# First attention of a two-block model: two of the convolution's four channel tiles move from VectorE to TensorE

## The reference, cut to what matters

```python
def conv_group(a, b, conv_w, conv_b, g_ln, b_ln):
    h = a * jax.nn.sigmoid(b)
    h = lax.conv_general_dilated(h, conv_w[:, None, :].astype(h.dtype), window_strides=(1,),
                                 padding=[(CONV_K - 1, 0)],
                                 dimension_numbers=('NWC', 'WIO', 'NWC'),
                                 feature_group_count=CONV_CH) + conv_b
    h = layernorm(h, g_ln, b_ln)
    return jax.nn.silu(h)
```

## Time and profile before

| what | us |
|---|---|
| three runs | 3038.69, 3042.77, 3051.34 |
| their median | 3042.77 |
| the profiled execution | 3043.8 |
| its span, first to last instruction | 3042.0 |
| mean granted TensorE clock | 0.955 |
| PE, DVE, ACT, POOL busy | 2918.6, 1798.2, 996.2, 989.8 |

### The profile page before, as it was taken

One profiled execution on the slowest core, in us unless ns is written; L12 is line 12 of the kernel. 1 busy time (PEld: TensorE's weight loads), 2 busy tenths in 40 slices (PEclk: granted clock), 3 DMA queues, 4 the chain that ended last, 5 costly groups with the idle time before them and its releaser, 6 DMA issues. The chain is left out here.

```text
span 3042.0 us, 39382 instructions
## 1 busy us (share of the span) xinstructions
PE 2918.6 (96%) x15042; PEld 2590.3 (85%) x15042; DVE 1798.2 (59%) x3227; ACT 996.2 (33%) x1582; POOL 989.8 (33%) x611
## 2 busy tenths in 40 slices
PE   8787999999999999999999999999999899999998
PEld 7555799999998999999998787888788898778886
DVE  6785876989798587888885833331043455333311
ACT  4345233343433322222223223222223456332222
POOL 3201500111202232233343544444432344454442
PEclk9766999999999999999999999999999799999999
DMA  3101256696969988989984322333331000223332
GB/s 133 32 1 35 84 155 202 214 289 192 288 205 297 358 317 317 329 320 324 325 320 138 101 93 83 97 97 100 96 130 37 4 1 15 76 83 97 97 104 70
DMA packets 195744, 475.83 MB, mean 156 GB/s; under 512 B 17204, under 2 KB 104116, under 8 KB 193252
## 3 DMA queue, kind: packets, MB, share of 16 engines
q1 hardware_dynamic: 167764, 370.54, 37.0%
q0 software_dynamic: 27648, 100.68, 9.6%
q10 hardware_dynamic: 144, 2.10, 0.2%
HBM read 415.47 MB, written 56.62 MB: 155 GB/s over the span
## 5 line engine op out<-in xcount | busy, mean ns | idle before, releaser
L262 ACT ACTIVATE w_hi<-w 128x1024 fp32r<-128x1024 f32 (+2 forms) x485 | 506.6, 1046 | 1235.9 <-DVE ffn_gates L2127 326.0
L272 POOL TENSOR_TENSOR w_lo<-w,w_hi 128x1024 fp32r<-128x1024 f32 (+2 forms) x229 | 542.9, 2383 | 698.0 <-ACT w_hi L262 698.0
L272 DVE TENSOR_TENSOR w_lo<-w,w_hi 128x1024 fp32r<-128x1024 f32 x256 | 313.5, 1225 | 177.5 <-ACT w_hi L262 150.5
L307 PE MATMUL peer_psum<-xn_hi,w_hi 128*128 128x416 f32 x1024 | 366.3, 358 | 1.7 <-ACT peer_act_out L1629 1.7
L307 PE MATMUL peer_psum<-peer_w_hi,w_hi 128*128 128x416 f32 x1024 | 359.6, 351 | 1.8 <-DVE peer_w_lo L404 1.1
L308 PE MATMUL peer_psum<-xn_lo,w_hi 128*128 128x416 f32 x1024 | 360.9, 352 | 0.0
L309 PE MATMUL peer_psum<-xn_hi,w_lo 128*128 128x416 f32 x1024 | 360.7, 352 | 0.0
L308 PE MATMUL peer_psum<-peer_w_lo,w_hi 128*128 128x416 f32 x1024 | 358.6, 350 | 0.0
L309 PE MATMUL peer_psum<-peer_w_hi,w_lo 128*128 128x416 f32 x1024 | 358.6, 350 | 0.0
L1465 POOL DMA_INDIRECT peer_gathered<-in_peer_u,peer_chosen_here x96 | 140.9, 1468 | 644.5 <-DVEq L1712 515.3
L307 PE MATMUL ffn_psum<-ffn_hn_hi,w_hi 128*128 128x512 f32 x704 | 277.2, 394 | 10.7 <-DVE ffn_hn_lo L617 6.6
(11 more groups left out here) (417 smaller groups left out, 5727.9 us busy)
## 6 DMA issues: line engine op xcount, KB each, us to landing
w<-in_peer_uT SPq DMA_DIRECT2D x128, 512.0 KB, 4.1
w<-in_peer_v SPq DMA_DIRECT2D x128, 512.0 KB, 5.5
w<-in_f_w_gu SPq DMA_DIRECT2D x88, 512.0 KB, 3.5
peer_act<-peer_act_out SPq DMA_DIRECT2D x128, 208.0 KB, 5.2
peer_gate<-peer_gates_out SPq DMA_DIRECT2D x26, 1024.0 KB, 7.8
peer_gates<-peer_gate SPq DMA_DIRECT2D x16, 1664.0 KB, 9.5
peer_act_in<-peer_act SPq DMA_DIRECT2D x128, 208.0 KB, 4.5
w<-in_f_w_down SPq DMA_DIRECT2D x32, 512.0 KB, 3.5
```

The costliest lines, as they stand in the source:

```text
L262: act.activation(self.hi[:, x, 0:c], self.buf[:, x, 0:c], ACT.Copy).then_inc(self.rounded, 1)
L272: eng.tensor_tensor(self.lo[:, x, 0:c], self.buf[:, x, 0:c], self.hi[:, x, 0:c].bitcast(F32), ALU.subtract).then_inc(self.split, 1)
L307: pe.matmul(out, w[0], x[0], start=start, stop=False)
```

## The change

Channel tiles 3 and 2 are taken from DVE. For each tap k of each, POOL makes a 128x128 matrix with the tap's weights on the diagonal (identity times weight per partition) into one of 8 buffers `diag`; PE multiplies it with the shifted input and accumulates the 31 taps of a tile in PSUM bank 6, all in fp32. Tile 3 comes first, tile 2 after it in the same bank.

- On PE the taps stand between the scores and the transposes of a step (`ahead`): three a step up to step 10, where the 31st is one alone, none in step 11, four a step from step 12 to 18 and three in step 19. Each waits for its diagonal (`diag_made`); tap 31, the first of the second tile, also for the eviction of the first (`tile_taken`).
- On POOL the 62 diagonals stand ahead of its two additions; from the ninth on each waits until the matmul 8 before it has run (`diag_used`).
- On DVE `take` moves the sum from bank 6 to the accumulator and adds the bias, in step 11 and in step 20. `Conv.run` leaves tiles 2 and 3 alone, in both stages. The front still does 25 taps, on tiles 0 and 1; 37 are left for this stage, so `per_step` is 2.

```diff
--- before.py
+++ after.py
@@ -653,7 +653,7 @@
     def run(self, dve, own, m, there=CT):
 
         for _ in range(m):
-            left = [c for c in range(there) if self.taps[c] < CK]
+            left = [c for c in range(min(there, CT - 2)) if self.taps[c] < CK]
             if not left:
                 return
             c = left[sum(self.taps) % len(left)]
@@ -970,7 +970,7 @@
         for i, it in enumerate(items):
             self.last[it["bank"]] = i
 
-    def on_pe(self, pe, between=None):
+    def on_pe(self, pe, between=None, ahead=None):
         it, s, n_items = self.items, self.s, len(self.items)
         for n in range(n_items + self.lag + 1):
             if n < n_items:
@@ -981,6 +981,8 @@
                     mm = pe.matmul(self.S[n % len(self.S)][:, col:col + keys.shape[-1]], x["q"], keys,
                                    start=True, stop=True)
                 mm.then_inc(s["scored"], 1)
+            if ahead is not None:
+                ahead(n)
             if self.lag <= n < n_items + self.lag:
                 m = n - self.lag
                 x = it[m]
@@ -1117,8 +1119,13 @@
                   lambda j: kit.gain("g_out_conv", j), ps[:, 6:7, :], 1, need=(silu_done, lambda j: j + 1),
                   bufs=ln.bufs)
         own_sem, conv_sem = st.sem("vector_steps"), st.sem("conv_steps")
+        DIAGS, on_tensor = 8, [(c, k) for c in (CT - 1, CT - 2) for k in range(CK)]
+        diag = st.sb("tap_diagonals", [P, DIAGS, P])
+        diag_made, diag_used = st.sem("diagonals_made"), st.sem("diagonals_used")
+        tile_taken = st.sem("tile_taken")
         conv_steps = 20
-        per_step = -(-(CK * CT - sum(conv.taps)) // conv_steps)
+        per_step = -(-(CK * (CT - 2) - sum(conv.taps)) // conv_steps)
+        assert conv.taps[CT - 1] == conv.taps[CT - 2] == 0
         first = conv_steps + 1
         with nc.Block() as block:
 
@@ -1136,11 +1143,30 @@
                     pe.wait_ge(centred, 1)
                     ln.on_pe(pe)
 
+                def tap(n):
+                    c, k = on_tensor[n]
+                    pe.wait_ge(diag_made, n + 1)
+                    if n == CK:
+                        pe.wait_ge(tile_taken, 1)
+                    pe.matmul(ps[:, 6, :], diag[:, n % DIAGS, :], io["conv_in"][:, c, NMETA + k:NMETA + k + SEQ],
+                              start=(k == 0), stop=(k == CK - 1)).then_inc(diag_used, 1)
+
                 steps = {first: mean, first + 4: sum_ln, first + 10: sum_cn}
-                at.on_pe(pe, lambda n: steps[n]() if n in steps else None)
+
+                def some_taps(n):
+                    done = 3 * n if n < 12 else CK + 4 * (n - 12)
+                    for k in range(done, min(done + 3, CK) if n < 12 else min(done + 4, 2 * CK)):
+                        tap(k)
+
+                at.on_pe(pe, lambda n: steps[n]() if n in steps else None, some_taps)
 
             @block.gpsimd
             def _(pool):
+                for n, (c, k) in enumerate(on_tensor):
+                    if n >= DIAGS:
+                        pool.wait_ge(diag_used, n - DIAGS + 1)
+                    pool.tensor_scalar(diag[:, n % DIAGS, :], kit.ident[:, :], kit.gain("conv_w", k * CT + c), None,
+                                       ALU.mult).then_inc(diag_made, 1)
                 pool.wait_ge(rows_squared, 2)
                 pool.tensor_tensor(io["attn_sum"][:, :], squares[:, 0, :], squares[:, 1, :], ALU.add).then_inc(rows_added, 1)
                 pool.wait_ge(rows_squared, 3)
@@ -1188,11 +1214,20 @@
                          first + 11: lambda: cn.variance(dve), first + 13: factor,
                          first + 14: lambda: cn.scale(dve, own, cn.src, cn.gain, None, cn.out)}
 
+                def take(i):
+                    c = on_tensor[i * CK][0]
+                    dve.wait_ge(diag_used, CK * (i + 1))
+                    dve.tensor_scalar(acc[:, c, :], ps[:, 6, :], kit.gain("conv_b", c), None, ALU.add).then_inc(tile_taken, 1)
+
                 def between(n):
+                    if n == 11:
+                        take(0)
                     if n < conv_steps:
                         conv.run(dve, taps, per_step)
                     if n == conv_steps:
                         taps.wait()
+                        take(1)
+                        dve.wait_ge(tile_taken, 2)
                         for c in range(1, CT):
                             if c > 1:
                                 dve.wait_ge(conv_done, c - 1)
```

## The result

The kernel after took 3055.66 us (median of 19 runs, 3046.91 to 3063.88), the kernel before 3041.22 us (19 runs on the same chips, 3032.59 to 3051.34). The ratio is 1.0047, with a 95% interval from 1.0036 to 1.0057: 14.4 us slower. The forecast was 17 us slower; its time of 3061 is 5 us above the measured one. The outcome lies just inside the 0.5% that the prediction called no change, so its likeliest class, slower by more than that, was missed by a hair, and the interval reaches across that line. One slow execution each of two later kernels (3527.56 us of "eight diagonals", 3686.82 us of "half the columns") is left out of their medians and ratios.

The account below looks back on a forecast made before the run. DVE's taps were taken to bound the first attention, PE at full clock afterwards. Taps 55.8 + attention 46.4 + 3 - 4 put score matmul 20 22.9 us later; less 5.9 behind it, +17 us: 3061 us, range 3045 to 3095.

Parts of the forecast that it names:

- likeliest class: Whole program: slower by more than about 0.5% (15 us), chance 0.66; same 0.28, faster 0.06.
- The bound changes sides: First attention to score matmul 20: 42 us leave DVE, which stops being the bound, and PE becomes it.
- The tap: One 128x128 by 512 fp32 matmul on PE at full clock: 0.90 us, 62 of them 55.8 us, bounds 53.0 and 58.9.
- Attention beside the taps: PE's attention until score matmul 20: about 18.3 steps of 2.54 us at full clock, 46.4 us.
- The start at half clock: First steps of the attention: full clock only from the second or third step on, costing 3 us more.
- the weight load in front of a short group: PE in steps to 20: a long tap ahead can hide a load of about 0.19 us; 4 us off, 0 to 8.
- The clock: PE in the attention with taps: full clock from the second or third step, 102 us instead of 201 at half.
- rival B: Clock stays at half for much of the attention stretch; 3077 to 3164 us, chance 0.18.
- The hidden parts: Attention steps: score chain, evictions and POOL's diagonals (0.45 us each) stay hidden behind PE; zero, at worst a few us.
- rival D: DVE and POOL block one another until POOL sets PE's pace, from 1.4 us a diagonal; no chance of its own.
- Behind step 20: Chain after score matmul 20: mean 4.1 us sooner, then 1.8 us less to DVE's mask of step 22; 5.9 us gained.
- A: The forecast case, PE bound at full clock: centre +17 us, 3045 to 3077 us, chance 0.72, two thirds above +15.

Follow-up runs that it names:

- eight diagonals: The kernel after, but POOL makes only the first 8 of the 62 diagonals and PE reuses them for all taps (wrong weights); 3052.49 us, ratio 1.0040 to before.
- half the columns: The kernel after with taps of 256 instead of 512 columns, DVE filling the second half with a copy (wrong values); 3031.41 us, ratio 0.9964 to before.
- Two taps: The kernel after with 60 of its 62 taps and diagonals left out, so the convolution's sum is incomplete; 3018.05 us, ratio 0.9931 to before.
- before again: The kernel before, unchanged, profiled a second time; 3044.94 us.
- the late idle matmuls: The kernel before plus unread 512-column matmuls, one in each of steps 16 to 19, two in steps 20 and 21; 3039.75 us, ratio 0.9996 to before.
- one tile: The kernel after with only tile 3 on PE: 3035.40 and 3032.96 us, 0.9975 to before; with 14 idle matmuls behind the taps 3026.18 and 3024.59 us.
- two tiles: The kernel after (62 taps on PE) plus idle matmuls in steps 24, 29, 30 and 31; 3060.08 us, ratio 1.0055 to before.
- diagonals twice: The kernel after with each diagonal made twice on POOL, the first time into a spare buffer; 3058.23 us, ratio 1.0063 to before.

## Why the prediction was right, point by point

**The bound changes sides: right.** DVE's 42 us came off it without shortening anything by themselves, and PE's taps set the pace. Half the columns show it one to one.

**The tap: 0.90 us forecast, 0.86 measured.** The prediction's lower bound, half of the half-clock row less its start (0.855), was the truth; I had leaned towards 0.95, a row in which PE partly waited. 62 x 0.04 = 2.5 us too much.

**Attention beside the taps.** Without them the stretch is 96.8 - 62 x 0.86 = 43.5 us, against 46.4 + 3 - 4 = 45.4. The start at half clock cost 1.8 us (4.85 from the first score matmul to the second, 3.02 for the next), not 3. That leaves 41.7 us for 18.3 steps, 2.28 a step, so 4.8 us came off and not 4. The size was right by luck, since the reason wasn't: I let a tap hide the weight load in front of a short group. "Two taps" has steps without one (PE there, then in after):

```profile
155.76 0.71 PE L981 MATMUL mla_psum<-kT,qT 96*128 96x16 f32 x4
156.67 0.73 PE L994 MATMUL mla_psum<-ident,mla_probs 128*128 128x128 f32 x5 [0.20 <-ACT mla_probsT L1041]
...
178.17 0.71 PE L981 MATMUL mla_psum<-kT,qT 96*128 96x16 f32 x4
178.72 0.71 PE L994 MATMUL mla_psum<-ident,mla_probs 128*128 128x128 f32 x5
...
208.19 0.71 PE L981 MATMUL mla_psum<-kT,qT 96*128 96x16 f32 x4
208.73 3.60 PE L1151 MATMUL mla_psum<-conv_in,mla_tap_diagonals 128*128 128x512 f32 x8
```

In step 17 the next group begins 0.55 us after the scores without a tap and 0.54 with four; the step takes 2.56 us (178.17 to 180.73), and in after 6.00 - 4 x 0.86 = 2.56. Where the steps differ, PE waits for ACT in "two taps" and not in after: step 9 takes 2.95 us there (155.76 to 158.71) and 5.14 - 3 x 0.86 = 2.56 in after. From step 8 to score matmul 20 that makes 31.1 us against 28.2. The brackets on those waits add up to 1.4 of the 2.9 us between; the rest lies in shorter gaps. One of the two steps in the earlier trace rows took 2.63 us where the same step in after takes 2.34. Together with the taps 4.4 us less than forecast: score matmul 20 came 96.8 us behind the first where 101.2 were forecast.

**The clock: right in its result, weak in its reason.** It was at 1.00 from 132 to 240 us, and rival B didn't occur. But the row from 140 to 164 at 0.50 carried more weight than it could bear: in "before again" and in "two taps" attention alone reached 1.00 within that window. I read one execution's place of the rise as a property of the work. The chance of 0.18 for B rested on it.

**The hidden parts: right.** The diagonals cost PE nothing (eight of 62: 96.80 us both times), though each took 0.60 us and more, not 0.45: the row of the same shape but another form of the instruction was no good price. The margin of rival D was real, and even pairs at 1.4 us cost only 3.3 us, at the start. Beside POOL two of DVE's taps took 1.52 us, 1.40 without it. The eviction at step 11 cost nothing. Taps of step 12 begin 0.97 us behind its scores as in other steps (179.66 - 178.69 and 185.21 - 184.24 in the timeline of PE).

**Behind step 20: -5.9 forecast, -7.9 or -6.2 measured,** depending on which profile of before is taken. The mean began 5.3 us behind score matmul 20, as forecast, and from it to DVE's mask of step 22 it took 232.00 - 229.75 = 2.25 us, 2.4 forecast. Both pieces fit. The second is a gain of the clock, but it can be lost behind: the late idle matmuls gave before the same piece and the stage nothing. The first, 4.1 us, was never tried by itself. Against before again the rest of the chain adds 0.1 us; against the first profile 1.8. A full clock through the rest, which the prediction bounded at 9 us, gave 5.5 at 0.91 with one tile. The change didn't bring it: the clock fell at about 240, once PE had waited 1.89 us for ACT in step 24, and again at about 261, behind a wait of 2.62 us.

**The sum.** 18.5 - 7.9 = +10.6 us for the stage between the two first profiles, +13.2 with the second one of before; +14.4 in the runs; +17 forecast. The steps that were mis-sized are the tap and the start, 2.5 and 1.2 us, and two thirds of A above the bound of 15 us was too bold for a centre at 17 with terms as uncertain as these.

## What to carry to other kernels

Work moved off a bound engine is worth only the distance to the next one: at full clock attention needs some 44 us of PE, so a stretch of 78 had room for 34, and 53 were put on it. Half the move (27 us) made the stretch 5 to 6 us shorter than before, where the whole one made it 19 longer; add up both engines for each split before choosing one. And when a later chain leaves the engine's clock low, a few matmuls that nobody reads can be worth as much as the move (some 8 us each, with one tile). With two tiles they were worth nothing in the total, for a reason not found, so it has to be tried in each kernel.

## What was unexpected of the hardware

- The same program was at the upper clock from 157 us on in one execution and still at the lower one at 164 in another, with the same work running; in "two taps" it rose at about 152 after 20 us of busy PE at 0.50.
- A matmul of 512 fp32 columns against 128x128 weights has a pitch of 0.86 us at 2.4 GHz, and one of 256 columns 0.43, back to back: half the columns, half the time. From a score matmul of 144 keys to the next group it is 0.54 us ahead of a tap (one tile, 188.65 to 189.19) and 0.55 ahead of transposes that are ready (two taps, 178.17 to 178.72), where before had 0.80 (190.06 to 190.86).
- POOL's `tensor_scalar` of 128x128 fp32 took 0.60 us with a scalar for each partition and 0.45 in the form of the earlier trace rows. Where DVE takes its taps at the same time both get longer: POOL's up to 1.12 us (147.62 in "diagonals twice", beside taps from 147.53 to 149.05), and DVE's pair 1.52 us in place of 1.40.
